# Seven places of a one-core decoder step: the order of x's first tile, one bank's evacuation, the chunk steps, the attention's first scores, the sample gates, and two rows of a fill table

## The reference

```python
def project(x, g_pre, w_in, pos):
    u = rmsnorm(x, g_pre) @ w_in          # 1024 -> q_m k_m v_m o_m z_m i_m f_m q_n kvc kvs kvw g_n z_n
...
def mlstm_group(...):                     # causal conv of width 4 and silu on q, k; gates ig, log-sigmoid fl
    h, C, n, m = mlstm_chunked(q, k, v, ig, fl, C0, n0, m0)
    # b = cumsum(fl); m_t = max(m_{t-1} + fl_t, ig_t); weights exp(log_d - m), state C, n, m
...
def nsa_core(...):                        # compressed, selected and window branch, each a masked softmax
    return gates[..., 0:1] * o_c + gates[..., 1:2] * o_s + gates[..., 2:3] * o_w
...
def merge(x, h_m, z_m, o_n, z_n, w_out, g_post):
    y = jnp.concatenate([h_m * jax.nn.silu(z_m), o_n * jax.nn.silu(z_n)], axis=-1) @ w_out
    return x + rmsnorm(y, g_post)
```

## Time and profile before

| | us |
|---|---|
| median of 3 timed runs | 1045.43 |
| lowest and highest | 1041.87, 1046.67 |
| the profiled execution | 1042.63 |
| its span in the trace | 1040.8 |
| TensorE busy in it | 1013.2 (97% of the span) |
| VectorE, ScalarE busy | 472.1 (45%), 337.9 (32%) |
| mean granted clock of TensorE | 0.991 of full |

### The profile page before, as it was taken

One profiled execution on the slowest core, in us unless ns is written; L12 is line 12 of the kernel. 1 busy time (PEld: TensorE's weight loads), 2 busy tenths in 40 slices (PEclk: granted clock), 3 DMA queues, 4 the chain that ended last, 5 costly groups with the idle time before them and its releaser, 6 DMA issues.

```text
span 1040.8 us, 14844 instructions
## 1 busy us (share of the span) xinstructions
PE 1013.2 (97%) x5419; PEld 603.2 (58%) x5419; DVE 472.1 (45%) x1171; ACT 337.9 (32%) x824; POOL 71.7 (7%) x179
## 2 busy tenths in 40 slices
PE   8999999999999999999999999999999999999997
PEld 6656654444445555569666545666666778445444
DVE  4285451000122222223153788878877476453452
ACT  5241110000001111111112677777777642122220
POOL 0000000000000001112101110000020430000000
PEclk9999999999999999999999899999999999999999
DMA  9232020020403115144200310000020678544412
GB/s 278 99 145 81 0 81 0 13 91 0 84 1 97 25 24 118 37 117 70 67 1 15 104 45 2 2 1 2 1 82 1 148 198 266 151 122 140 144 50 78
DMA packets 86246, 77.52 MB, mean 74 GB/s; under 512 B 28358, under 2 KB 71666, under 8 KB 86110
## 3 DMA queue, kind: packets, MB, share of 16 engines
q1 hardware_dynamic: 74558, 61.84, 20.3%
q10 hardware_dynamic: 11616, 14.74, 5.8%
HBM read 66.59 MB, written 14.10 MB: 78 GB/s over the span
## 4 chain that ended last, share of the span: by engine, by line
PE 90%; DVE 4%; ACT 2%; DMA 1%; SPq 1%; issue 1%; DVEq 0%; ACTq 0%
PE PS L2267 29%; PE PS L2257 14%; PE PS L2514 10%; PE PS L2338 7%; PE PS L2351 6%; PE PS L2323 6%; PE PS L2182 3%; PE PS L2164 1%; DMA WR<-in_w_in 1%; PE PS L2543 1%; PE PS L2210 1%; PE PS L2265 1%; PE PS L2113 1%; PE PS L2126 1%; PE PS L2123 1%
## 5 line engine op out<-in xcount | busy, mean ns | idle before, releaser
L2267 PE MATMUL PS<-WR,XT 128*128 128x512 f32 (+1 forms) x768 | 306.9, 557 | 0.0
L2267 PEld LDWEIGHTS PS<-WR,XT 128*128 128x128 f32 x768 | 144.0, 190 | 147.7 <-issue 144.6
L2257 PE MATMUL PS<-XT,WR 128*128 128x352 f32 x576 | 176.6, 465 | 2.6 <-ACT SQK L1047 2.0
L2257 PEld LDWEIGHTS PS<-XT,WR 128*128 128x128 f32 x576 | 108.7, 191 | 61.7 <-ACT SQK L1047 2.6
L2323 PE MATMUL PS<-KTR,XT 64*128 64x512 f32 (+3 forms) x352 | 71.1, 509 | 0.0
L1229 ACT ACTIVATE XT<-XT 128x640 f32<-128x640 f32 (+7 forms) x96 | 69.8, 731 | 2.8 <-DVE XT L1700 2.7
L2338 PE MATMUL PS<-cst,XT 128*128 128x128 f32 x396 | 65.0, 288 | 5.0 <-DVE XT L1711 3.8
L1700 DVE CUSTOM_DVE_ANT_1 XT<-PS,KVN 128x640 f32<-128x640 f32 (+6 forms) x84 | 62.1, 764 | 16.8 <-PE PS L2323 16.7
L2338 PEld LDWEIGHTS PS<-cst,XT 128*128 128x128 f32 x396 | 42.4, 141 | 41.9 <-issue 18.1
L2514 PE MATMUL PS<-WR,QT 128*128 128x512 f32 x128 | 61.2, 599 | 0.0
L2514 PE MATMUL PS<-WR,KT 128*128 128x512 f32 x128 | 60.7, 597 | 0.0
(11 more groups left out here) (478 smaller groups left out, 1199.1 us busy)
## 6 DMA issues: line engine op xcount, KB each, us to landing
WR<-in_w_in SPq DMA_DIRECT2D x24, 512.0 KB, 6.3
WR<-in_cache_kv_cmp SPq DMA_DIRECT2D x56, 128.0 KB, 2.5
MT<-row_factors ACTq DMA_DIRECT2D x16, 256.0 KB, 7.3
WR<-in_w_in SPq DMA_DIRECT2D x32, 128.0 KB, 3.3
QN<-in_cache_kv_win SPq DMA_DIRECT2D x8, 512.0 KB, 5.2
out_s_kv_win<-in_cache_kv_win SPq DMA_DIRECT2D x1, 4064.0 KB
out_y_prompt<-MT ACTq DMA_DIRECT2D x7, 512.0 KB, 2.9
XT<-in_x_prompt ACTq DMA_DIRECT2D x6, 512.0 KB, 4.3
```

The lines of the kernel that those rows point to most:

```text
L2257: ins = mm(b[:, 0:THIRD], w[:, k, u * P:(u + 1) * P], xt[:, k, third * THIRD:(third + 1) * THIRD], **f)
L2267: ins = mm(b[:, 0:width], xt[:, k, r * P:(r + 1) * P], w[:, k, :], **f)
```

## The change

- x's first tile is scaled ahead of the parameters on DVE, the second ahead of the first tile's `turn_in`; the multiplies of `warm` are 10, 0, 2, 5, 6 in place of 8, 6, 10, 0, 5 around the same transposes; the two bias rows no longer count for `params_in` but for `rest_in`.
- SP loads w_in's second 128 columns behind x's tile 4 in place of behind the samples' tile; the second tile of the projection waits for these alone, the tile r = 6 for the other two quarters.
- `take_third(1, 2)`, which empties the bank of tile 5, stands behind the first of the four gate exponentials in place of behind the last.
- `mstep` leaves the short sample tiles out: the 24 steps stand behind the 24 full tiles.
- `scores(1)` stands ahead of the wait for the last evacuations and of `aux(0, 3)`; `qks` stands behind the first pair's scaling; its tanh on ACT stands at tile r = 6 of z_n.
- The samples' cumulative sum and running maximum are one scan each (`tensor_tensor_scan`) over 32 columns in place of twelve short instructions; three short ones and a memset of one column set up the restart at each sequence. The constant table grows by 32 columns.
- `FILL`: 3 and 3 multiplies at `gates` and `cmp` of the first group in place of 2 and 4; 4 at `u8` and 7 at `q2` of the second group in place of 2 and 9.

```diff
-    return 16 * sum(2 * KC if GROUPS[m][0] in ("q_n", "z_n") else 4 if m else 3 for m in range(g % 2, g + 1, 2))
+    return 16 * sum(2 * KC if GROUPS[m][0] in ("q_n", "z_n") else 4 if m else 2 for m in range(g % 2, g + 1, 2))
...
-                 "u8": 2, "u9": 2, "u10": 2, "u11": 2, "q2": 9, "pt0": 4, "pt1": 6, "pv1": 4}]
+                 "u8": 4, "u9": 2, "u10": 2, "u11": 2, "q2": 7, "pt0": 4, "pt1": 6, "pv1": 4}]
...
-        STEP0 = first_tile(5)
-
         def mstep(n):
-            k = n - STEP0
-            return (k % 3, k // 3) if 0 <= k < 3 * NT else None
+            g, r = tile_of(n)
+            k = (g - 5) * NT + r
+            return (k % 3, k // 3) if 5 <= g < 8 and r < NT else None
...
-            for i in range(3, NT + 1):
+            load_x(3)
+            load_x(4)
+            sp.dma_start(w0[:, :, P:2 * P], w[:, :, P:2 * P]).then_inc(x_in[5], 16)
+            for i in range(5, NT + 1):
                 load_x(i)
-            for u in range(1, 4):
+            for u in range(2, 4):
...
-            act.dma_start(bias_i[0:MH, :], I["b_igate"].rearrange("l h -> h l")).then_inc(params_in, 16)
+            act.dma_start(bias_i[0:MH, :], I["b_igate"].rearrange("l h -> h l")).then_inc(rest_in, 16)
...
+                if r == 6:
+                    act.wait_ge(s_conv_done, 1)
+                    nc.scalar.activation(ctmp_s, accs, ACT.Tanh).then_inc(s_tanh_done, 1)
...
+            scale_in(0)
             take_parameters()
-            scale_in(0)
+            scale_in(1)
             turn_in(0)
-            scale_in(1)
             scale_in(2)
...
-            dve.wait_ge(s_tanh_done, 1)
-
-            dve.wait_ge(proj_done, ALL)
-            nc.vector.scalar_tensor_tensor(qks, ctmp_s, 1.0, accs, op0=ALU.add, op1=ALU.mult).then_inc(s_qk_ready, 1)
-
...
             for h in range(KVH):
                 scale(0, h)
+            dve.wait_ge(s_tanh_done, 1)
+            nc.vector.scalar_tensor_tensor(qks, ctmp_s, 1.0, accs, op0=ALU.add, op1=ALU.mult).then_inc(s_qk_ready, 1)
...
-            link(nc.vector.tensor_copy(b4(b_s)[:, :, 0], b4(fl_s)[:, :, 0]))
-            for t in range(1, ST):
-                link(tt(b4(b_s)[:, :, t], b4(b_s)[:, :, t - 1], b4(fl_s)[:, :, t], ALU.add))
+            link(nc.vector.tensor_tensor_scan(b_s, s_col(S_REST, NS)[0:MH, :], fl_s, 0.0, ALU.mult, ALU.add))
+            link(tt(a_s, rows[:, 0, :], b_s, ALU.subtract))
+            link(tt(b4(r_s)[:, :, 0], b4(fl_s)[:, :, 0], m0[0:MH, :], ALU.add))
+            link(tt(b4(rows[:, 0, :])[:, :, 0], b4(rows[:, 0, :])[:, :, 0], b4(r_s)[:, :, 0], ALU.max))
+            link(nc.vector.memset(b4(fl_s)[:, :, 0], -3e38))
+            link(nc.vector.tensor_tensor_scan(m_s, fl_s, rows[:, 0, :], 0.0, ALU.add, ALU.max))
             sum_sample(2, (1,))
-            for t in range(ST):
-                link(tt(b4(m_s)[:, :, t], b4(fl_s)[:, :, t], b4(m_s)[:, :, t - 1] if t else m0[0:MH, :], ALU.add))
-                link(tt(b4(m_s)[:, :, t], b4(m_s)[:, :, t], b4(rows[:, 0, :])[:, :, t], ALU.max))
-            link(tt(a_s, rows[:, 0, :], b_s, ALU.subtract))
...
+            scores(1)
             pe.wait_ge(evac_act, evacuated(ALL - 1, "act"))
             pe.wait_ge(evac_dve, evacuated(ALL - 1, "dve"))
             aux(0, 3)
-            scores(1)
```

More of the change, by code:

```diff
@@ L88 @@
 S_PAIR = S_SAME + P
-S_END = S_PAIR + 4
+S_REST = S_PAIR + 4
+S_END = S_REST + NS
 def constant_tables():
@@ L127, in constant_tables @@
     s[:, S_PAIR:S_PAIR + 4] = p[:, None] % NS // ST == 4 * (p[:, None] // NS) + np.arange(4)[None, :]
+    s[:, S_REST:S_REST + NS] = k[None, :] % ST != 0
     s[:, S_SAME:S_SAME + P] = p[:, None] % NS == p[None, :] % NS
@@ L551, in build @@
         SIGNAL = {"gates": 1, "cmp": 2, "imp": 3, "ct": 4, "new": 5, "pt0": 6, "pt1": 7, "pv0": 8, "pv1": 9, "o": 10}
-        FILL = [{"gates": 2, "cmp": 4, "u0": 1, "u1": 2, "u2": 2, "u3": 2, "q0": 2, "u4": 2, "u5": 2, "ct": 1, "u6": 2, "u7": 2, "new": 3,
+        FILL = [{"gates": 3, "cmp": 3, "u0": 1, "u1": 2, "u2": 2, "u3": 2, "q0": 2, "u4": 2, "u5": 2, "ct": 1, "u6": 2, "u7": 2, "new": 3,
                  "u8": 2, "u9": 2, "u10": 2, "u11": 2, "q2": 9, "pt0": 4, "pt1": 6, "pv1": 4, "o": 2},
                 {"gates": 2, "cmp": 4, "u0": 1, "u1": 2, "u2": 2, "u3": 2, "q0": 2, "u4": 2, "u5": 2, "ct": 1, "u6": 2, "u7": 2, "new": 3,
[1 row of a table removed]
[1 row of a table added]
         OUT_ORDER = [(0, h, c) for h in range(2) for c in range(6)] + [(0, h, c) for h in range(2) for c in (6, 7)] \
@@ L1072, in _ @@
             nc.scalar.activation(g4[64:64 + MH, :], gm_m, ACT.Exp, scale=-1.0)
+            take_third(1, 2)
             act.wait_ge(gates_in, 3)
@@ L1077, in _ @@
             nc.scalar.activation(dec_rows[0:MH, :], wkc[0:MH, :], ACT.Exp).then_inc(gates_exp, 1)
-            take_third(1, 2)
             act.wait_ge(gates_exp, 2)
@@ L1218, in _ @@
                     aux_act(0, 1)
-            act.wait_ge(s_conv_done, 1)
-            nc.scalar.activation(ctmp_s, accs, ACT.Tanh).then_inc(s_tanh_done, 1)
             def exps(p, h):
@@ L1443, in _ @@
             turn_in(NT)
-            dve.wait_ge(rest_in, 2 * 16)
+            dve.wait_ge(rest_in, 4 * 16)
             nc.vector.tensor_copy(masks[:, :], cst[:, 0:K_MT]).then_inc(xt_ready, 1)
@@ L2051, in _ @@
             pe.wait_ge(zeros_ready, 2)
-            warm(8)
+            warm(10)
             pe.wait_ge(x_in[0], 2 * 16)
-            pe.wait_ge(params_in, 5 * 16)
+            pe.wait_ge(params_in, 3 * 16)
             nc.tensor.transpose(bank(4)[:, 0:48], par_rows[0:48, :], ident[0:48, 0:48]).then_inc(x_turned, 1)
-            warm(6)
-            turn_x(0)
-            warm(10)
-            turn_x(1)
-            turn_x(2)
-            warm(5)
+            turn_x(0)
+            warm(2)
+            turn_x(1)
+            warm(5)
+            turn_x(2)
+            warm(6)
             def free_bank(n):
@@ L2248, in _ @@
                     if g == 0 and r == 1:
+                        pe.wait_ge(x_in[5], 2 * 16)
+                    if g == 0 and r == 6:
                         pe.wait_ge(w_in_s[0], weights_in(0))
```

7 lines of the change are left out of this document (3 added, 4 removed).

## The result

The changed kernel takes **1031.77 us** (1031.09 to 1032.66, four runs) against 1046.05 (1041.87 to 1047.35, four runs) for the one before: ratio 0.989, 95% interval 0.986 to 0.991, faster by 0.9 to 1.4%. The profiled executions were 1031.09 against 1042.63, with spans of 1029.3 against 1040.8: 11.5 us. The sum of 12.2 was a sum over one trace, so I hold it against the 11.5 of the traces.

What follows compares the result with a forecast made beforehand. PE was taken to set the end, so gains must come from its idle time or clock. Six terms summed to 12.2 us: 1030.4 from the profiled 1042.63, 1031.8 from the middle 1044.0; stated 1031.5, range 1026.5 to 1039.5.

Steps and rivals of the forecast that it cites:

- The sum of 12.2: Whole kernel: gains of six places added, 3.1 + 1.9 + 2.4 + 1.5 + 1.7 + 1.6 us; chance 0.50.
- The gate's bank: q_m: tile 9's wait goes, tile 10 waits 1.85 us instead, clock stays up; gain 1.9 us, bounds 0 and 2.1.
- The chunk steps: Stage 2 behind full tiles: two waits of 1.18 us go; gain 2.4 us, bounds 0 and 2.4.
- the sample gates: Samples' gates: twelve short instructions become five, PE's wait of 1.72 us goes; gain 1.7 us, bounds 1.2 and 1.9.
- `u8` and `q2`: Second group's fill table: two more multiplies fill PE's 1.66 us wait at `u10`; gain 1.6 us, bounds 0 and 1.7.
- rival (d): Chunk steps: chunk 6's row factors starve, stage 1 stands 17 us, kernel slower at 1048.8 us; chance 0.04.
- The start: Kernel's start: first product at 13.9 in place of 17.05; gain 3.1 us, bounds 1.4 and 3.5.
- my lower bound of 1.4: The start: least gain expected there, 1.4 us, against 3.1 taken.
- My sign for a late clock: The start: a first product at 15 or later would say that the clock was the step that failed.
- the 13.9 of my walk: The start: time in us of the first product, from following DVE through the new order; 3.1 us sooner.
- The attention: Attention's start: earlier `scores(1)` and later `qks`, first half-clock stretch goes, second stays; gain 1.5 us, bounds 0.5 and 4.
- rival (b): Attention's start: both half-clock stretches go, another 2.5 us gained, 1029.2 us; chance 0.14.

Runs made afterwards that it cites:

- all_filled: Changed kernel with idle multiplies in the start's two idle stretches and the third pair's wait, and `qks` ahead of the maxima again: 1027.71 us.
- start_before: Changed kernel with the old start (order of loads, parameters ahead of the first scaling, both gate biases waited for, old warm multiplies): 1033.83 us.
- start_filled: Changed kernel with the two idle stretches of PE's start filled with idle multiplies: 1030.84 us.
- gate_before: Changed kernel with tile 5's evacuation behind all the exponentials again: 1032.59 us.
- before_busy: Kernel before, with four identity multiplies inside the wait ahead of tile 9 of q_m and nothing else: 1042.06 against 1043.18 us.
- after_again: Changed kernel run once more, unchanged, for a second profiled execution: 1032.21 us.
- scores_before: Changed kernel with the second pair's scores behind the last evacuation again, `qks` left where it is: 1034.04 us.
- qks_before: Changed kernel with `qks` ahead of the first maxima on DVE again: 1031.20 us.
- att_filled: Changed kernel with five identity multiplies inside the wait ahead of the third pair's transpose in the attention's start: 1029.11 us.
- filled_chunk_before: all_filled with the chunk steps placed as before, also behind the short tiles: 1030.83 us.
- filled_samples_fill_before: all_filled with the samples' gates in single steps and both tables of fillings as before: 1033.27 us.
- before_filled: Kernel before, with identity multiplies ahead of tile 9 of q_m (four) and in the third pair's wait (five): 1039.39 against 1043.83 us.

## Why the prediction was right, and where it wasn't

**The time and the sign** were right: 1031.5 forecast, 1031.77 measured. The sum behind it was right in four terms of six, in one of the four by luck.

**The gate's bank, 1.9.** The mechanism and the number came as said: wait at tile 10, 1.84 us, clock up. That the number fits is luck: the term rests on a fall of the clock that I called "likely but not certain", and took as certain in the sum. The runs have the wait of 2.03 to 2.04 at tile 9 twice, once with the fall and once without. The wait alone is worth 0.2.

**The chunk steps, 2.4; the sample gates, 1.7; `u8` and `q2`, 1.6.** Measured 2.4, 1.6 and 1.7 in the first pair of traces, and again 2.4, 1.6 and 1.7 when they were undone on all_filled. These are waits read off one line each, with DVE's or the transfers' slack behind them walked out. The row factors of chunk 6 took 10.2 us from issue to use for the 10.5 of chunk 7, so rival (d) never came near. The scans took 0.21 and 0.47 for my 0.2 each, in each of the executions whose trace has them; with it the wait for the block sums grew from 0.51 to 0.84, more than the 0.2 that I had allowed. Why the second is longer isn't shown. Short instructions without a scan do it there as well (before's L1781 on 4x8 took 0.52 once and 0.16 otherwise), so it need not be the half throughput that the Trainium skill gives the scan ("DVE: opcode table, instruction layouts, handler registers and perf-mode slots", section 6).

**The start, 3.1, was the step that failed.** I wrote that PE "works without a gap from about 7.5". It stood for 1.16 us from 9.3 on, because ACT began x's second tile at 7.87, where the trace of before had it at 6.44, though nothing ahead of it in the queue had changed. And I had taken the clock for full behind the idle time that ends at 7.33; it was half for 6.8 us. The pair shows 0.75 us at the first product and 0.9 once x's tiles are through, under my lower bound of 1.4. My sign for a late clock, a first product at 15 or later, came (16.30), but it can't tell the clock from a late tile. Over all profiled executions (in brackets, when ACT began x's second tile):

| start | first product (second tile) | mean |
|---|---|---|
| old | 16.83 (6.20), 17.05 (6.44), 18.30 (6.66), 19.05 (8.09) | 17.8 |
| new | 13.99 (6.75), 14.27 (6.22), 14.85 (6.71), 16.30 (7.87), 16.38 (8.00), 16.66 (7.76) | 15.4 |
| new, filled | 13.85 (6.82), 13.87 (6.83), 13.94 (6.90), 14.52 (7.48) | 14.0 |

In all four filled starts the first product stands 7.03 to 7.04 us behind ACT's begin of the second tile: with PE busy, and a tile begun between 6.82 and 7.48, the tile alone sets it. So of the 2.45 us from 13.85 to 16.30, 1.05 is the later tile (7.87 for 6.82), and the other 1.4, by this estimate, is the clock's and PE's. The new start is worth 2.4 us on average, and the 13.9 of my walk is what it gives when PE stays busy and the tile is there by 6.9. I had compared a full-clock walk with one quick execution of the old start.

**The attention, 1.5,** was too small by 1.6. The part that I walked out came: the lead grows by 1.7, from 5.2 to 6.9, up to the third pair's transpose (574.15 for 581.06). Its cause was only partly right: `scores(1)` is worth 1.1, while moving `qks` beside it costs 0.2; which of `qks` and the first half-clock stretch was worth the other 0.6 in before's order isn't separated. The other 1.4 us are the second half-clock stretch, 3.4 us long for 6.9; that was halfway to rival (b). Undoing `scores(1)` did not bring a stretch back in the one execution traced, so which stretches an execution has is not fixed by these waits alone. Half-clock time in the attention, in the order of the executions:

| wait of 1.6 ahead of the third pair | half-clock time, 560 to 600, us |
|---|---|
| idle | before 10.2, after 3.4, start_before 3.4, start_filled 10.2, gate_before 13.6, before_busy 10.2, after_again 3.4, scores_before 0, qks_before 3.4 |
| filled | att_filled 0, all_filled 0, filled_chunk_before 3.4, filled_samples_fill_before 3.4, before_filled 3.4 |

With the wait filled no stretch begins behind it; the three that are left lie in front. **Shown**, for the changed kernel, is that filling this idle time takes away the long stretches and with them the long times. **Open** is what decides between 3.4 and 13.6 us, and what the stretches in front hang on.

**The two errors cancelled,** which the agreement of 1031.5 with 1031.77 hides: the start's shortfall of 2.2 and the attention's excess of 1.6.

## What to carry to other kernels

A wait that ends on one line of the profile is worth what the line says, and it is safe to add such terms; a half-clock stretch read from one execution is not, since the next execution may have none or twice as much, so look at several before you put it in a sum. Where the engine that sets the end must stand for over a microsecond, idle multiplies into the bank that it is about to write are worth trying before the wait itself is attacked: here five of them gained 3.1 us, as much as the largest of the edits, and made the times repeat within 1 us in five executions (2.1 in the five of all_filled). Such an idle time can also hide a late transfer: compare the distance from the transfer's use to what hangs on it, as with x's second tile, before blaming the clock. When two instructions are moved together, undo each alone: one of the pair here was a loss of 0.2 by the traces.

## What the runs showed of the hardware

- **The clock's falls are drawn anew in each execution.** In five executions whose idle times at the attention's start agree within 0.01 us (after, start_before, start_filled, gate_before, after_again), 3.4, 3.4, 10.2, 13.6 and 3.4 us at half clock followed. The Trainium skill ("TensorE: Matmul & The Clock Gate", part 1) says that the same kernel starts with a different number of slow multiplies from run to run. The new start agrees: the ten passes behind tile 1's transposes took 2.39 to 2.51 us in five executions and 1.38 in one.
- **The clock's record can miss the start.** A pass of an idle multiply lasts 0.14 us at full clock (ten in 1.38) and 0.25 at half (ten in 2.51). In after_again four took 1.22 at 8.38, and the trace's first record of the clock is of 10.6 us. The Trainium skill ("TensorE: Matmul & The Clock Gate", part 1) says that these records have been seen to be unreliable and asks for a cross-check; here they were missing where the durations tell of a slow clock.
- **Half clock also followed short idle times close together, at times.** The stretch at 562.6 came behind 0.6 and 0.4 us of idle time, and that at 570 in the kernel before behind 1.1 and 0.8; with the same idle times the clock stayed full in all_filled and scores_before. The single wait of 1.84 or 1.85 at tile 10 was followed by full clock in all ten executions that have it.
- **The same transfers land at different times:** x's second tile was begun by ACT at 6.20 to 8.09 us over the fourteen traces, behind the same two transfers of its queue.
